# A two-block transformer forward pass: a query norm folded into its scores, a last norm by halves, two moved steps

## The reference

```python
# block 1: three mixers, merged and projected, then product-key experts
x  = x + merged @ w_out
h2 = rmsnorm(x, g_ffn)                      # x * rsqrt(mean(x^2) + eps) * g
q  = h2 @ w_q                               # 8 heads, 2 halves of 128
sc = einsum(q, sub_keys)                    # scores, then top 16 twice, softmax
x  = x + experts(h2, top_i, softmax(top_v)) # all expert rows of u times h2, gelu, times v
x  = rmsnorm(x, g_final)
# block 2
h = rmsnorm(x, norm_mix[0]); x = x + gated_delta(h)
h = rmsnorm(x, norm_mlp[0]); x = x + relu(h @ w1)**2 @ w2
h = rmsnorm(x, norm_mix[1]); x = x + dilated_window_attention(h)
h = rmsnorm(x, norm_mlp[1]); x = x + relu(h @ w1)**2 @ w2
out = rmsnorm(x, norm_final)
```

## Time and profile before

| what | value |
|---|---|
| time, median of 3 | 1965.24 us (1965.13 to 1965.91) |
| the profiled execution's own time | 1967.95 us |
| its span, first to last instruction | 1966.2 us |
| mean granted TensorE clock, share of full | 0.98 |
| busy: PE, DVE, ACT, POOL | 95%, 66%, 46%, 1% |
| HBM traffic | 306.84 MB read, 157 GB/s over the span |

### The profile page before, as it was taken

The page is one execution under the profiler, slowest core; times in us unless marked ns, Lnnn a source line. Parts: engine busy times, 40 slices in busy tenths (PEclk is TensorE's granted clock), DMA queues, the critical chain, the costliest instruction groups (busy, mean ns, idle before and its releaser), DMA issues. The chain is left out here.

```text
span 1966.2 us, 31427 instructions
## 1 busy us (share of the span) xinstructions
PE 1875.1 (95%) x13051; PEld 1735.9 (88%) x13051; DVE 1290.5 (66%) x2042; ACT 899.6 (46%) x1169; POOL 18.1 (1%) x24
## 2 busy tenths in 40 slices
PE   7999898999999999999999989979899999999997
PEld 7998897899999999988888879868899889789986
DVE  5656874799688888755555557986566355446643
ACT  6457532243434343444444446665355343435532
POOL 0000000000000000000000000000000001000000
PEclk9999899999999999999999989987999999999999
DMA  6443354354444444465555543310254547515453
GB/s 226 171 172 135 113 187 172 129 174 173 153 150 147 151 149 151 172 224 192 192 192 192 192 156 129 129 65 23 87 174 168 203 185 213 134 73 186 178 191 119
DMA packets 44741, 310.66 MB, mean 158 GB/s; under 512 B 5166, under 2 KB 5678, under 8 KB 8144
## 3 DMA queue, kind: packets, MB, share of 16 engines
q1 hardware_dynamic: 42576, 303.58, 42.7%
q0 software_dynamic: 1472, 4.86, 1.5%
q10 hardware_dynamic: 576, 0.55, 0.1%
HBM read 306.84 MB, written 2.13 MB: 157 GB/s over the span
## 5 line engine op out<-in xcount | busy, mean ns | idle before, releaser
L310 DVE TENSOR_TENSOR s_ring_lo<-s_ring,s_w_hi 128x2048 fp32r<-128x2048 f32 x236 | 540.5, 2290 | 234.2 <-ACT s_w_hi L304 229.5
L304 ACT ACTIVATE s_w_hi<-s_ring 128x2048 fp32r<-128x2048 f32 x235 | 448.1, 1907 | 140.4 <-PE bank L347 65.2
L347 PE MATMUL bank<-s_hT_hi,s_w_hi 128*128 128x256 f32 x2000 | 288.5, 287 | 1.9 <-ACT s_w_hi L304 1.6
L347 PE MATMUL bank<-s_hT_hi,s_ring_lo 128*128 128x256 f32 x2000 | 281.9, 284 | 1.0 <-DVE s_ring_lo L310 0.8
L347 PEld LDWEIGHTS bank<-s_hT_hi,s_w_hi 128*128 128x128 f32 x2000 | 259.2, 193 | 6.7 <-issue 5.4
L347 PEld LDWEIGHTS bank<-s_hT_hi,s_ring_lo 128*128 128x128 f32 x2000 | 258.8, 193 | 1.8 <-DVE s_ring_lo L310 1.8
L1633 PE MATMUL bank<-s_w_hi,s_hT_lo 128*128 128x512 f32 x1008 | 238.8, 389 | 0.3 <-issue 0.3
L1633 PEld LDWEIGHTS bank<-s_w_hi,s_hT_lo 128*128 128x128 f32 x1008 | 189.2, 188 | 39.6 <-issue 0.4
L347 PE MATMUL bank<-s_hT_lo,s_w_hi 128*128 128x256 f32 x1040 | 147.4, 285 | 0.0
L347 PEld LDWEIGHTS bank<-s_hT_lo,s_w_hi 128*128 128x128 f32 x1040 | 135.7, 194 | 0.0
L347 PE MATMUL bank<-s_x_r,s_w_hi 128*128 128x256 f32 x960 | 134.8, 283 | 0.0
(11 more groups left out here) (435 smaller groups left out, 2440.5 us busy)
## 6 DMA issues: line engine op xcount, KB each, us to landing
s_ring<-weights SPq DMA_DIRECT2D x282, 1024.0 KB, 4.8
s_arena<-bias_by_distance POOLq DMA_DIRECT2D x12, 384.0 KB, 7.2
s_arena<-mem SPq DMA_DIRECT2D x1, 1024.0 KB, 6.0
s_x<-x SPq DMA_DIRECT2D x1, 1024.0 KB, 13.9
x_away<-s_x SPq DMA_DIRECT2D x1, 1024.0 KB, 4.8
s_arena<-sub_keys SPq DMA_DIRECT2D x1, 1024.0 KB, 7.1
s_arena<-x_away SPq DMA_DIRECT2D x1, 1024.0 KB, 6.8
out<-s_x SPq DMA_DIRECT2D x1, 1024.0 KB, 4.0
```

Of the source, the lines that this page charges most:

```text
L304: act.activation(k.w_hi[:, u % 2, :], k.ring[:, u % RING, :], ACT.Copy).then_inc(k.hi_ready, 1)
L310: dve.tensor_tensor(k.ring_lo[:, u % RING, :], k.ring[:, u % RING, :], plain(k.w_hi[:, u % 2, :]), ALU.subtract).then_inc(k.lo_ready, 1)
L347: last = pe.matmul(out[:, nb * S:(nb + 1) * S], w[:, c, nb * P:(nb + 1) * P], h[:, c, :], start=(n == 0 and c == 0), stop=(n == 2 and c == 7))
```

## The change

It has four parts.

1. **Queries from x without its norm's root.** `normalise` is gone. A `QuerySeam` turns x itself: three quarters inside `merge`, each behind an out unit, and the fourth at the head of `peer`. ACT copies the turned x times the norm's weights into hT and squares the quarters. The query units read this hT, which lacks each token's inverse root. The root is put into the scores as the scale of ACT's copy, now two copies of 256 columns in place of one of 512. For the experts the root is needed in h: PE spreads it over the partitions by two small products after the second query unit (L1664 of the new kernel), ACT copies that out, DVE multiplies hT by it into `scaled` (2048 columns), ACT rounds this to the high half and DVE makes the low half ahead of the second head's search. ACT copies `scaled` back to hT after the third expert unit.
2. **Last norm by halves.** `normalise_rows` and `store` are gone. `LastNorm` runs inside the last `mlp`, one 128-token tile after the other, in halves of 512 columns; each tile is stored by a DMA of its own, 512 KB. The norm's weights are loaded amid the ring's loads of the last feed-forward.
3. **Weighing between turnings.** In the dilated attention `turn(j)` is cut for j from 1 to 5: two groups, then `weigh(j - 1)`, then the third. ACT's copies are cut alike.
4. **A low half moved.** `split_lo` of the first unit of the gated rule stood on DVE ahead of the adds to x after the experts; it now stands behind `factors`.

Two groups of semaphores are also freed at the heads of two earlier blocks instead of together after `merge`.

```diff
+class QuerySeam(Seam):
+    def __init__(self, k, gcol, banks):
+        Seam.__init__(self, k, gcol, banks)
+        k.doubles += 1
+        k.queries += 1
+        self.sums, self.mean, self.inverse, self.roots = (
+            k.small[:, a:b] for a, b in ((32, 40), (40, 42), (42, 44), (44, 46)))
+        self.spread, self.one = k.slots[:, 0, :], k.slots[:, 1:3, 0:P]
+    def copy(self, act, j):
+        act.wait_ge(self.k.x_turned, self.at + j + 1)
+        for c in range(2):
+            n = 2 * j + c
+            last = act.activation(self.k.hT[:, n, :], self.k.ps[self.banks[j]][:, c * S:(c + 1) * S], ACT.Copy,
+                                  scale=self.gcol[:, n:n + 1])
+        last.then_inc(self.k.x_rounded, 1)
+    def squares(self, act, junk, j):
+        act.wait_ge(self.k.x_added, self.at + j + 1)
+        for tt in range(TT):
+            last = act.activation(junk[:, j, tt, :], self.k.x[:, tt, j * S:(j + 1) * S], ACT.Square,
+                                  accum_out=self.sums[:, 4 * tt + j:4 * tt + j + 1])
+        return last
...
-def normalise(k, src, gcol, dstT, lay_at, split=None):
...
+class LastNorm:
...
+    def squares(self, act, half, tt):
+        act.wait_ge(self.added, self.at + 2 * half + tt + 1)
+        act.activation(self.junk[:, tt, half, :], self.k.x[:, tt, half * 512:(half + 1) * 512], ACT.Square,
+                       accum_out=self.sums[:, 2 * tt + half:2 * tt + half + 1]).then_inc(self.squared, 1)
+    def weigh(self, dve, half, tt):
+        at = slice(half * 512, (half + 1) * 512)
+        dve.wait_ge(self.added, self.at + 2 * half + tt + 1)
+        dve.tensor_tensor(self.w[:, tt, at], self.k.x[:, tt, at], self.g_rows[:, at], ALU.mult)
+    def inverse_mean(self, dve, own, tt):
+        one = slice(tt, tt + 1)
+        dve.wait_ge(self.squared, self.squares_at + 3 + tt)
+        own.up(dve.tensor_tensor(self.mean[:, one], self.sums[:, 2 * tt:2 * tt + 1],
+                                 self.sums[:, 2 * tt + 1:2 * tt + 2], ALU.add))
+        own.settle(dve)
+        own.up(dve.tensor_scalar(self.mean[:, one], self.mean[:, one], 1.0 / D, EPS, ALU.mult, ALU.add))
+        own.settle(dve)
+        dve.reciprocal(self.inverse[:, one], self.mean[:, one]).then_inc(self.mean_ready, 1)
+    def take_root(self, act, tt):
+        act.wait_ge(self.mean_ready, self.steps_at + tt + 1)
+        act.activation(self.root[:, tt:tt + 1], self.inverse[:, tt:tt + 1], ACT.Sqrt).then_inc(self.root_ready, 1)
+    def scale_left(self, dve, tt):
+        dve.wait_ge(self.root_ready, self.steps_at + tt + 1)
+        dve.tensor_scalar(self.k.x[:, tt, 0:512], self.w[:, tt, 0:512], self.root[:, tt:tt + 1], None,
+                          ALU.mult).then_inc(self.scaled, 1)
+    def scale_right(self, act, tt):
+        act.wait_ge(self.root_ready, self.steps_at + tt + 1)
+        act.activation(self.k.x[:, tt, 512:D], self.w[:, tt, 512:D], ACT.Copy,
+                       scale=self.root[:, tt:tt + 1]).then_inc(self.scaled, 1)
+    def store(self, sp):
+        for tt in range(TT):
+            sp.wait_ge(self.scaled, 2 * (tt + 1))
+            sp.dma_start(self.k.out[tt * P:(tt + 1) * P, :], self.k.x[:, tt, :]).then_inc(self.k.x_saved, 16)
+        sp.wait_ge(self.k.x_saved, 48)
...
-def normalise_rows(k, src, g_dram, dst):
...
                 unit_N_split(k, pe, U["out"] + n, merged_r, [bank[:, 0:S], bank[:, S:2 * S]])
+                seam.turn(pe, n - 1)
...
+            seam.copy(act, 0)
+            seam.squares(act, junk, 0)
+            seam.copy(act, 1)
+            seam.squares(act, junk, 1)
+            seam.squares(act, junk, 2)
+            seam.copy(act, 2)
...
             split_lo(k, dve, F + 9)
-            split_lo(k, dve, F + 10)
-            split_lo(k, dve, F + 11)
             dve.wait_ge(k.unit_done, U["out"] + 1)
             for tt in range(TT):
                 xs = k.x[:, tt, 0:S]
-                own.up(dve.scalar_tensor_tensor(out=xs, in0=out_first[tt], scalar=0.5, in1=xs,
-                                                op0=ALU.mult, op1=ALU.add))
+                last = dve.scalar_tensor_tensor(out=xs, in0=out_first[tt], scalar=0.5, in1=xs, op0=ALU.mult,
+                                                op1=ALU.add)
+            last.then_inc(k.x_added, 1)
+            split_lo(k, dve, F + 10)
             for n in range(1, 4):
                 dve.wait_ge(k.unit_done, U["out"] + n + 1)
                 xs = k.x[:, :, n * S:(n + 1) * S]
-                own.up(dve.scalar_tensor_tensor(out=xs, in0=halves(out_bank[n][:, :]), scalar=0.5, in1=xs,
-                                                op0=ALU.mult, op1=ALU.add))
+                dve.scalar_tensor_tensor(out=xs, in0=halves(out_bank[n][:, :]), scalar=0.5, in1=xs, op0=ALU.mult,
+                                         op1=ALU.add).then_inc(k.x_added, 1)
+                if n == 1:
+                    split_lo(k, dve, F + 11)
...
+        begin.turn(pe, 3)
+        pe.wait_ge(k.x_rounded, begin.at + 4)
         for h in range(PEER_H):
             if h >= 2:
                 pe.wait_ge(q_out, h - 1)
             unit_T(k, pe, Q + h, k.hT, ps[h % 2])
+            if h == 1:
+                pe.wait_ge(k.scaled, TT * k.norms + 1)
+                for tt in range(TT):
+                    last = pe.matmul(ps[4][:, tt * P:(tt + 1) * P], k.ones, begin.one[:, tt, :], start=True, stop=True)
+                last.then_inc(k.turned, 1)
             if h >= 1:
                 score(h - 1)
...
-        act.activation(flat(k.hT_hi), flat(k.hT), ACT.Copy).then_inc(k.rounded_out, 1)
+        begin.copy(act, 3)
+        begin.squares(act, junk, 3).then_inc(k.squares, 1)
+        act.wait_ge(k.mean_ready, k.norms + 1)
+        act.activation(begin.roots, begin.inverse, ACT.Sqrt).then_inc(k.root_ready, 1)
+        act.wait_ge(k.root_ready, k.norms + 1)
         for h in range(PEER_H + 1):
             if h < PEER_H:
                 act.wait_ge(k.unit_done, Q + h + 1)
                 act.activation(qT[:, 2 * h:2 * h + 2, :], halves(ps[h % 2][:, :]), ACT.Copy).then_inc(q_out, 1)
             if h >= 1:
                 act.wait_ge(score_mm, h)
-                act.activation(sc[:, h - 1].rearrange("p t q k -> p (t q k)"), ps[2 + (h - 1) % 2][:, :],
-                               ACT.Copy).then_inc(score_out, 1)
+                for tt in range(TT):
+                    last = act.activation(sc[:, h - 1, tt].rearrange("p q k -> p (q k)"),
+                                          ps[2 + (h - 1) % 2][:, tt * S:(tt + 1) * S], ACT.Copy,
+                                          scale=begin.roots[:, tt:tt + 1])
+                last.then_inc(score_out, 1)
+            if h == 1:
+                act.wait_ge(k.turned, 4 * k.norms + 1)
+                act.activation(begin.spread, ps[4][:, 0:S], ACT.Copy).then_inc(query_spread, 1)
+            if h == 2:
+                act.wait_ge(query_scaled, 1)
+                act.activation(flat(k.hT_hi), flat(scaled), ACT.Copy).then_inc(k.rounded_out, 1)
...
+            if j == 2:
+                act.activation(flat(k.hT), flat(scaled), ACT.Copy).then_inc(scaled_here, 1)
...
-        dve.wait_ge(k.rounded_out, k.rounds + 1)
-        k.rounds += 1
-        dve.wait_ge(k.x_saved, 16)
-        dve.tensor_tensor(k.x_r[:, :], flat(k.hT), plain(flat(k.hT_hi)), ALU.subtract).then_inc(h_split, 1)
+        def factor():
+            dve.wait_ge(k.squares, TT * k.norms + 1)
+            own.up(dve.tensor_reduce(begin.mean, begin.sums.rearrange("p (t n) -> p t n", t=TT), AX.X, ALU.add))
+            own.settle(dve)
+            own.up(dve.tensor_scalar(begin.mean, begin.mean, 1.0 / D, EPS, ALU.mult, ALU.add))
+            own.settle(dve)
+            dve.reciprocal(begin.inverse, begin.mean).then_inc(k.mean_ready, 1)
+            dve.wait_ge(k.root_ready, k.norms + 1)
+            for tt in range(TT):
+                last = dve.tensor_scalar(begin.one[:, tt, :], k.ident, begin.roots[:, tt:tt + 1], None, ALU.mult)
+            last.then_inc(k.scaled, 1)
+        factor()
+        dve.wait_ge(query_spread, 1)
+        dve.tensor_tensor(scaled, k.hT[:, :, :], over(begin.spread, KC), ALU.mult).then_inc(query_scaled, 1)
         for h in range(PEER_H):
+            if h == 1:
+                dve.wait_ge(k.rounded_out, k.rounds + 1)
+                dve.wait_ge(k.x_saved, 16)
+                dve.tensor_tensor(k.x_r[:, :], flat(scaled), plain(flat(k.hT_hi)), ALU.subtract).then_inc(h_split, 1)
             dve.wait_ge(score_out, h + 1)
...
         downs(dve, body)
-        split_lo(k, dve, U["gdn_qkv"])
...
         seam.factors(dve, own)
+        split_lo(k, dve, U["gdn_qkv"])
...
+        if ending:
+            ending.squares(act, 0, 0)
+            ending.squares(act, 0, 1)
+            for tt in range(TT):
+                ending.squares(act, 1, tt)
+                ending.take_root(act, tt)
+                ending.scale_right(act, tt)
...
+        if ending:
+            dve.wait_ge(k.g_here, 32)
```

(50 more changed lines are left out.)

173 lines of the change are left out of this document (50 added, 123 removed).

## The result

The changed kernel takes 1956.23 us (median of 7 executions, 1951.26 to 1959.03); the kernel before, beside it, 1965.49 (7, 1963.60 to 1970.35). The ratio is 0.9947, 95% interval 0.9937 to 0.9958: faster by 0.53%, 9.3 us between the medians, where 16.2 were forecast. The profiled execution took 1956.48, with a span of 1954.7.

What follows compares the result with a forecast made beforehand. PE was busy for 95% of the span, so time is won only where it stands still or runs at the low clock. Gains of 6.3 + 5.4 + 3.1 + 1.4 = 16.2 us gave 1965.2 - 16.2 = 1949.0 us, range 1946.0 to 1954.0.

Steps and rivals of the forecast that it cites:

- The terms at their places: Gains at the start of the queries, 6.3 us; the end, 5.4; the dilated attention, 3.1; the double norm, 1.4.
- the sum: Over the whole kernel the four local gains add up to 16.2 us less time.
- The first rival: At the head of the queries, new pauses drop the clock to 1.2 GHz, giving 1950.8 to 1952.0 us; 15%.
- The rule that I weighed: At the start of the queries, transposes don't count as PE activity, so the new queries would begin at 1.2 GHz.
- The other rivals: Dilated attention loses its 3.1 us (8%); DVE's later search costs 5.7 (8%); slower than before, 1968.2 (3%).
- Part 3 does what it says: Its rival: in the dilated attention ACT's exponentials may hold the copies, so 3.1 us is lost: 1952.1; 8%.
- The search is hidden: DVE's search, 5.7 us later, ends within idle time before the experts; the rival, not hidden, gives 1954.7; 8%.

Runs made afterwards that it cites:

- without part 4: The changed kernel with the low half back at its old place: 1947.46 us, beside 1964.41 for the kernel before.
- the column beside it: Stretches of the trace of the changed kernel with the low half back at its old place, against the kernel before; its median time was 1947.46 us.
- filling: Products whose results nobody reads, put into four of PE's short waits in the changed kernel: 1947.30 us, beside 1964.41 for the kernel before.
- part 4 alone: The kernel before with only the low half moved behind the factors: 1970.57 us, beside 1964.41 for the kernel before.
- part 3 alone: The kernel before with only the weighing put between the turnings of the dilated attention: 1964.81 us, ratio 0.9988 to the kernel before.
- a shift of 1.44 us: The changed kernel with 12 products nobody reads before the eleventh expert unit: 1947.79 us, beside 1964.98 for the kernel before.

## Why the prediction was wrong

**The terms at their places were right.** Read from the stretches, against the forecast: part 1, 6.3 forecast; 7.84 - 0.69 - 0.86 for the two turns that now stand before 305 = 6.3 us, in the trace without part 4, which has full clock there. Part 2, 5.4 forecast, 5.9 measured over the stretch (5.8 of it from the last add to the end, 11.9 to 6.15; a store of 512 KB took 2.6 where I had 2.9). Part 3, 3.1 forecast, 3.3 measured. Part 4, 1.4 forecast, 1.38 and 1.39 measured. Sum 16.9.

**The step that failed is the sum.** "6.3 + 5.4 + 3.1 + 1.4 = 16.2" was set against the rest of the kernel as if the rest kept its length; outside the seam, a change of the clock in untouched work was put at nothing, without a reason. It isn't nothing: in these traces the granted clock falls for some microseconds after some of PE's waits and thin stretches, and whether it falls depends on the moment at which they come. Each gain moves all the work behind it. In the changed kernel's trace the terms gave 16.9 us, and the work up to 290, ahead of the first edit on PE, was 2.0 shorter by chance; lost were 1.65 at the head of the queries, 0.3 at the first expert unit (330 to 1150 against the column beside it), 2.3 in the gated rule and 3.05 in the dilated attention, 7.3 in all, which leaves the measured 11.5 of span within 0.1. From 1172 to 1290 it was as slow as before's trace, where the trace without part 4 is 3.4 us faster. The share of part 4 is measured: not 1.4 us of gain but a loss of 7 to 9 within the changed kernel, and of some 6 alone. What it does there is to move the work to another moment; its order by itself is not the cause.

**The first rival had the mechanism, and the wrong reach.** I gave 15% to "the clock falls at the seam" and priced it there only, 1.8 to 3. The seam cost 1.65, and the clock fell at it in four of the seven traces that have the new seam unfilled, so 15% was too little. I took the clock as a risk of the places that were edited, when more was lost behind them, in the gated rule and at the first dilated scores, which nobody edited; and I had read the mean clock of 0.98 on the page and not asked where the missing 2% lay.

**The rule that I weighed** did not decide it. In the changed trace the clock fell behind two waits with four transposes between; in the trace without part 4 it stayed at 1.00 through the same waits and the same transposes. The Trainium skill (TensorE: Matmul & The Clock Gate, Part 4: PE-mode transpose) says that transposes don't count as PE-busy in the same way; as I had applied that rule, both should have fallen.

**The other rivals.** Part 3 does what it says. The search is hidden. Of the 13 executions of the changed kernel the longest took 1959.23, 3.1 us less than the shortest of before beside any kernel here (1962.30).

**What stays open.** Why these distances are good and others bad isn't shown; they are read off the traces, for this kernel, and which one an execution meets was not controlled. At the double norm 1.4 us earlier is bad and 1.4 later than that good again. Whether filling helps by itself wasn't parted: the seam was at full clock in three unfilled traces too. And executions of one kernel still spread by 2 to 11 us.

## What to carry to other kernels

Small gains at single places of a long program on PE can't be added when it has stages in which the clock falls: read each gain at its place by lining up the instructions of two traces, and then see where the granted clock was low in code that nobody touched. When a local gain appears in the trace and not in the time, shift the work behind it by a microsecond of harmless products before blaming the edit. Then look for the same low stretch in kernels with and without the edit, and see how far the work stands from the last change of the clock. And judge such a change by the times of many executions with their mean clock, not by one profile, and not by the median alone where the times form groups.

## What was not expected of the hardware

Over all 156 executions of all thirteen kernels (before and twelve changed ones), with one constant for each kernel, each microsecond spent at the granted clock of 0.5 goes with 0.38 us of time, and what is left over scatters by 0.7 us only. The low time is worked out as 2 x (1 - mean clock) x span: 56 us without part 4, 73 before, 81 in the changed kernel, 85 with part 4 alone. At equal low time part 3 alone is worth 3.0 us, as at its place, though the medians differ by 0.6; the whole change 12.4 (I take it that some of the low time of before lay in waits that parts 1 and 2 removed, and cost nothing there; this wasn't tested). So the clock goes with almost all of the spread between executions, and a shift of 1.44 us moved the changed kernel's median by 8.7.
